# A streamed product-key layer: 84 tokens by index instead of 80, four row blocks instead of eight, a third of v in one fp32 pass

## The reference

```
q = (x @ w_q).reshape(T, 8, 2, 128)
s = einsum('thpd,pnd->thpn', q, sub_keys)         # 128 keys on either side
... top 16 of each side, top 16 of their sums     # 8 heads x 16 = 128 experts for each token
a  = gelu(einsum('td,tkd->tk', x, u[experts])) * gates
y  = einsum('tk,tkd->td', a, v[experts])          # u, v: 16384 rows of 1024, for each layer
```

## Time and profile before

| | us |
|---|---|
| median of 3 runs | 1576.46 (1574.13 to 1580.11) |
| the profiled execution: time | 1579.14 |
| the profiled execution: span | 1577.3 |
| TensorE busy | 1549.5 (98%) |
| VectorE busy | 1355.4 (86%) |
| ScalarE busy | 629.8 (40%) |
| GpSimd busy | 606.9 (38%) |

### The profile page before, as it was taken

How to read it: one execution, slowest core, us unless ns; L and a number is a source line. 1 busy time by engine, 2 the same in 40 slices (tenths; PEclk the granted TensorE clock), 3 DMA queues, 4 the chain that set the end, 5 groups by cost and what they waited for, 6 DMA issues and landing times. The chain is left out here.

```text
span 1577.3 us, 28052 instructions
## 1 busy us (share of the span) xinstructions
PE 1549.5 (98%) x10766; PEld 1494.5 (95%) x10766; DVE 1355.4 (86%) x2569; ACT 629.8 (40%) x1157; POOL 606.9 (38%) x438
## 2 busy tenths in 40 slices
PE   8999999999999999999999999999999999999998
PEld 8988999999999999999888899999999999999996
DVE  6987997989998998888956779898999888888895
ACT  4563222333334444544635341233333344444452
POOL 5651005644442555454003200265444435555520
PEclk9999999999999999999999999999999999999999
DMA  7644579999999999999833247799999999999990
GB/s 244 237 137 135 189 222 359 376 395 372 372 383 378 372 406 408 403 404 404 315 113 109 79 133 254 266 388 375 379 384 376 374 361 409 406 404 407 403 366 27
DMA packets 136965, 493.95 MB, mean 313 GB/s; under 512 B 16064, under 2 KB 16576, under 8 KB 136576
## 3 DMA queue, kind: packets, MB, share of 16 engines
q1 hardware_dynamic: 85248, 307.42, 52.3%
q0 software_dynamic: 47552, 170.06, 27.9%
q10 hardware_dynamic: 4032, 14.68, 2.6%
HBM read 488.79 MB, written 1.05 MB: 311 GB/s over the span
## 5 line engine op out<-in xcount | busy, mean ns | idle before, releaser
L690 POOL DMA_INDIRECT big<-v,picks x160 | 259.0, 1619 | 262.8 <-DVE big L1952 206.5
L690 POOL DMA_INDIRECT big<-u_rows,picks x160 | 220.4, 1377 | 245.9 <-DVE big L1868 217.3
L624 DVE TENSOR_TENSOR low<-raw,high 128x1024 fp32r<-128x1024 f32 x176 | 220.3, 1255 | 38.3 <-ACT high L1262 33.3
L728 PE MATMUL work<-columns,raw 128*128 128x176 f32 x1600 | 249.0, 313 | 3.2 <-DVE big L1846 3.2
L728 PEld LDWEIGHTS work<-columns,raw 128*128 128x128 f32 x1600 | 240.2, 190 | 3.7 <-issue 3.7
L1262 ACT ACTIVATE high<-raw 128x1024 fp32r<-128x1024 f32 x192 | 200.5, 1047 | 40.4 <-PE work L793 9.9
L1952 DVE SCALAR_TENSOR_TENSOR big<-big,side_hid 128x1024 f32<-128x1024 f32 x156 | 199.5, 1279 | 2.3
L1868 DVE SCALAR_TENSOR_TENSOR big<-big 128x1024 f32<-128x1024 f32 x160 | 190.4, 1218 | 9.3 <-DMA big<-u_rows,picks 9.3
L728 PE MATMUL work<-columns,extra_raw 128*128 128x176 f32 x1088 | 174.6, 317 | 5.0 <-DVE big L1846 4.3
L1530 ACT ACTIVATE xT<-big 128x176 fp32r<-128x176 f32 x198 | 67.5, 349 | 268.5 <-PE work L873 204.6
L728 PEld LDWEIGHTS work<-columns,extra_raw 128*128 128x128 f32 x1088 | 166.3, 193 | 5.5 <-issue 4.6
(11 more groups left out here) (262 smaller groups left out, 2881.8 us busy)
## 6 DMA issues: line engine op xcount, KB each, us to landing
raw<-u SPq DMA_DIRECT2D x150, 512.0 KB
raw<-v SPq DMA_DIRECT2D x146, 512.0 KB
extra_raw<-v SPq DMA_DIRECT2D x110, 512.0 KB
extra_raw<-u SPq DMA_DIRECT2D x106, 512.0 KB
raw<-wq SPq DMA_DIRECT2D x32, 512.0 KB
raw<-conv_in SPq DMA_DIRECT2D x14, 512.0 KB
aux<-ln_par ACTq DMA_DIRECT2D x9, 512.0 KB, 8.8
raw<-conv_out SPq DMA_DIRECT2D x8, 512.0 KB
```

What stands on the lines that cost most here:

```text
L624: ops.tensor_tensor(low_at(c), raw_at(c), high_at(c).bitcast(F32), ALU.subtract).then_inc(low_made[RAW_SLOT[c]], 1)
L690: nc.gpsimd.indirect_dma_start(out=side_rows[n % SIDE_BUFS], out_offset=None, in_=rows, in_offset=bass.IndirectOffsetOnAxis(ap=pick_ids[:, ...
L728: mm = nc.tensor.matmul(out_, raw_at(c)[:, k * P:(k + 1) * P], x_full[:, k, :], start=(k == 0), stop=(k == KD - 1))
```

## The change

It moves four tokens (`DT` 172) from the streamed to the gathered side. The second set has 20 tokens in six groups, and 128 experts in six groups make 22 gathers, the last not full; 120 of its 128 partitions are used, and the indices of the other eight are zero. Gathers for each layer go from 80 + 80 to 86 + 86. The batches of gates stay 22, the last with half its tokens left out. `TAIL` goes from 8 to 4, so four blocks of v for each layer are taken as column blocks instead of in rows. Every third block of v is whole (39 instead of 29), and 29 instead of 27 pairs of u. What each part computes stays the same.

```
-SETS = ((64, 2), (16, 8))
+SETS = ((64, 2), (20, 6))
-SET_ROWS = [PH * TOPK // _groups for _, _groups in SETS]
+SET_ROWS = [-(-PH * TOPK // _groups) for _, _groups in SETS]
+SET_USED = [_n * _groups for _n, _groups in SETS]
-BATCHES = DT // BATCH
+BATCHES = -(-DT // BATCH)
+GT = BATCH * BATCHES
-FULL_PAIRS = {5, 14, 23, 33, 42, *PAIR_OF}
+FULL_PAIRS = {5, 12, 18, 25, 33, 40, 47, *PAIR_OF}
-TAIL = 8
+TAIL = 4
-FULL_V = [_n for _n in range(FIRST_COLUMNS, COLUMNS - LAST_COLUMNS) if _n % 4 == 3]
+FULL_V = [_n for _n in range(FIRST_COLUMNS, COLUMNS - LAST_COLUMNS) if _n % 3 == 1]
-TURN_AFTER = (4, 2)
+TURN_AFTER = (4, 3)
+def pick_pieces(i, g):
+    lo, hi = SET_ROWS[i] * g, min(SET_ROWS[i] * (g + 1), PH * TOPK)
+    return [(a, b) for a, b in ((lo, min(hi, P // 2)), (max(lo, P // 2), hi)) if a < b]
...
+            nc.gpsimd.memset(picks[:], 0.0).then_inc(side_filled, 1)
+            nc.gpsimd.memset(side_hid[:], 0.0).then_inc(side_filled, 1)
...
             def add_sides(m):
-                for pick, total in zip(selector, side_sum):
-                    nc.tensor.matmul(y[:, 2 + m, :], pick, total[:, m * 512:(m + 1) * 512],
+                for pick, total, used in zip(selector, side_sum, SET_USED):
+                    nc.tensor.matmul(y[:, 2 + m, :], pick[0:used], total[0:used, m * 512:(m + 1) * 512],
...
             def combine_tail(first, norm, wait_block, wait_half=None):
+                count, slot = (TAIL, COLUMNS) if norm % 2 == 1 else (KD, 0)
```

More of the change, by code:

```diff
@@ L97 @@
 assert len(BATCH_OF) == BATCHES and len(SIDE_SUMS_AT) == SIDE_ROWS
+def pick_pieces(i, g):
+    lo, hi = SET_ROWS[i] * g, min(SET_ROWS[i] * (g + 1), PH * TOPK)
+    return [(a, b) for a, b in ((lo, min(hi, P // 2)), (max(lo, P // 2), hi)) if a < b]
+PICK_LOADS = [sum(len(pick_pieces(_i, _g)) for _g in range(SETS[_i][1])) for _i in range(len(SETS))]
 def set_of(d):
@@ L287, in gated_tokens @@
 def gated_tokens(pair):
-    return BATCH * sum(p <= pair for p in PAIR_OF)
+    return min(DT, BATCH * sum(p <= pair for p in PAIR_OF))
 def program(nc, x_rows, x_cols, positions, conv_par, diag, mla_par, ln_par, keys, w_uq, w_uk, w_uv,
@@ L667, in _ @@
                 pool.wait_ge(own_picked, layer + 1)
+                pool.wait_ge(side_filled, 2)
                 def fetch_picks(i, g):
[L670 to L674, removed]
+                    n, first_row = SETS[i][0], SET_ENDS[i] - SET_ROWS[i]
+                    for a, b in pick_pieces(i, g):
+                        half, to = divmod(a, P // 2)[0], first_row + a - SET_ROWS[i] * g
+                        at = a - half * (P // 2)
+                        nc.gpsimd.dma_start(
+                            picks[n * g:n * (g + 1), :, to:to + b - a],
+                            own_picks[SET_AT[i]:SET_AT[i] + n, :, half, at:at + b - a]).then_inc(picks_in[i], 16)
                 def fetch_tokens(i, g):
@@ L683, in _ @@
                     fetch_tokens(0, g)
-                pool.wait_ge(picks_in[0], 16 * SETS[0][1] * (layer + 1))
+                pool.wait_ge(picks_in[0], 16 * PICK_LOADS[0] * (layer + 1))
                 def gather(n):
@@ L924, in combine_tail @@
             def combine_tail(first, norm, wait_block, wait_half=None):
+                count, slot = (TAIL, COLUMNS) if norm % 2 == 1 else (KD, 0)
                 def part(n, halves, sides=range(2)):
-                    return combine_block(n, first + n, n == 0, n == TAIL - 1, halves, sides)
-                for n in range(TAIL):
+                    return combine_block((slot + n) % KD, first + n, n == 0, n == count - 1, halves, sides)
+                for n in range(count):
                     wait_block(first + n)
@@ L931, in combine_tail @@
                         pe.wait_ge(columns_sum, KD * (norm // 2) + 2)
-                    if norm % 2 == 1 and n == TAIL - 1:
+                    if norm % 2 == 1 and n == count - 1:
                         pe.wait_ge(columns_sum, KD * (norm // 2 + 1))
@@ L937, in combine_tail @@
                 mm.then_inc(y_half, 1)
-                combine_second_half(part, norm, range(TAIL), TURN_AFTER[min(norm, 1)], wait_half)
+                combine_second_half(part, norm, range(count), TURN_AFTER[min(norm, 1)], wait_half)
             def turn_part(n, h, part):
@@ L1936, in combine @@
                     step(V.memset(selector[i], 0.0))
[L1937 to L1938 removed]
+                    used = n * groups
+                    last = V.tensor_reduce(selector[i][0:used, SET_AT[i]:SET_AT[i] + n],
+                                           ident[0:used, 0:used].rearrange("p (g t) -> p t g", t=n), AX.X, ALU.add)
                 last.then_inc(selector_ok, 1)
                 def side_weighted(d):
[L1942 to L1943 removed]
+                    used = SET_USED[set_of(d)]
+                    n, total = before + SIDE_ROWS + d, side_sum[set_of(d)][0:used]
+                    weight = side_hid[0:used, d:d + 1]
                     if d == 0:
```

32 lines of the change are left out of this document (16 added, 16 removed).

## The result

The changed kernel takes 1590.47 us (median of 5, 1588.51 to 1593.67) beside 1578.15 of the kernel before (5 runs on the same chip): ratio 1.0081 [1.0065, 1.0097]. It is 0.8% slower. The forecast was 1563.3 us, faster, and its range ended at 1578: the kernel went the other way and past the end of the range. The profiled span went from 1577.3 to 1588.2 us.

What follows compares the result with a forecast made beforehand. The prediction took TensorE, 98% busy, as the bound, with the DMA engines close behind. Terms -20.0 (TensorE), +1.0 (end of layer 0) and +5.8 (DMA) sum to -13.2 us: 1563.3 us, own range 1556 to 1568, with rivals 1556 to 1578.

Steps and rivals of the forecast that it cites:

- TensorE, four tokens fewer: Matmuls in u and v: 0.053 us less for a whole block, 0.027 for a split one, narrow matmuls unchanged.
- no effect: Rival for TensorE's matmuls: 172 columns take the time of 176, so TensorE gains nothing; 1578 us, chance 0.05.
- v rows: Row stage of v: four row blocks become column blocks, each saving 0.61 us, -2.4 us a layer.
- The end of layer 0: Layer 0 to the next: fewer row matmuls hide the turn of x, so its first matmuls wait about +1.0 us.
- The DMA engines in v: Blocks 4 to 113 of v: 6.9 us missing a layer at 411 GB/s, reserve covers 4.0, +5.8 us in all.
- no reserve: Rival in v: all 6.9 us missing a layer show, +13.8 instead of +5.8; 1571.3 us, chance 0.20.
- 423 GB/s: Rival in v: the engines carry the wanted 423 GB/s, so nothing is missing; 1557.5 us, chance 0.17.
- 402 is the limit: Rival in v: 402 GB/s is all the engines carry, 12.5 us over TensorE's time; 1582.5 us, chance 0.12.
- VectorE in u: Stage u: VectorE's load grows +1.9 us on 174 of 190 us, hidden by TensorE's pace, at no cost.
- The DMA engines in u: Stage u: six more transfers on 185, 381 becomes about 400 GB/s, under 411, with no loss.
- VectorE becomes the bound in u: Rival in u: +1.9 us a layer at 91% busy doubles the 7.5 us of waits; 1571 us, chance 0.06.
- all hidden: Rival in v: the engines carry 423 GB/s or the reserve is 6.9 us; 1557.5 us, chance 0.17.

Runs made afterwards that it cites:

- before_quarter_narrow: The kernel before, with every fourth gather (20 of 80 in either pass) bringing 256 B a partition; 1577.57 us, ratio 0.9992.
- quarter_narrow: The changed kernel with every fourth gather (21 of 86 in either pass) bringing 256 B a partition; 1570.99 us, ratio 0.995.
- kinds_alone: The kernel before with only the new choice of whole blocks in u and v, old sets and eight row blocks; 1585.71 us, ratio 1.0048.
- six_narrow: The changed kernel with six of the 86 gathers of either pass bringing 256 B a partition instead of 4 KB; 1577.47 us, ratio 0.9993.
- half dots: The changed kernel, all gathers whole, with dots over 512 of the 1024 channels; 1578.45 us, ratio 0.9996.
- quarter_narrow_short_dots: The changed kernel with every fourth gather at 256 B a partition and dots over 512 of the 1024 channels; 1555.5 us, ratio 0.9847.
- after_half_gathers: The changed kernel with every gather after the first five of a layer bringing 64 of 128 partitions' rows; 1701.17 us, ratio 1.0782.
- after_gather_120: The changed kernel with the second set's 22 gathers bringing only the 120 used rows; 1694.95 us, ratio 1.073.
- after_late_set: The changed kernel with the second set's small loads issued from gather 30 on instead of 8; 1585.54 us, ratio 1.0043.

## Why the prediction was wrong

**TensorE, four tokens fewer: right where TensorE was free to show it.** A whole block in v, with its first split one:
```profile
1301.04 1.36 PE L898 MATMUL y<-big,extra_raw 128*128 128x172 f32 x8
...
1303.28 0.91 PE L885 MATMUL y<-xT,high 128*128 128x344 f32 x4
...
1305.53 0.83 PE L885 MATMUL y<-xT,high 128*128 128x344 f32 x4
```
The whole block takes 2.24 us and the next 2.25, where the earlier trace rows had 2.29 and 2.26: 0.05 and about 0.01 less in this place (0.053 and 0.027 forecast). Over the whole stage, v columns without the stall (before_quarter_narrow and quarter_narrow) went from 270.3 to 276.6 and 276.3, +6.3 and +6.0; the forecast was -2.5 and four blocks of 2.18 more, +6.2. The rival "no effect" is out.

**v rows: right.** 10.9 us less, 11.2 forecast. Kinds: right in v, as kinds_alone shows; in u VectorE paid for them, and the clock hid it.

**The end of layer 0: about right.** L854 starts at 805.72 after the rows' last matmul of about 805.1, 0.6 us late; 1.0 forecast.

**The DMA engines in v: the deficit was right, the reserve wrong.** The forecast had 6.9 us missing in each layer at 411 GB/s and 4.0 of them covered by slots. The stall is 283.2 - 276.6 = 6.6 and 283.1 - 276.3 = 6.8: the cover gave 0.3 and 0.1. At the 409 GB/s that were reached the same sum has 8.2 us missing, and the cover gave 1.6 and 1.4. Either is below the 1.8 that the forecast took as the least. The rival "no reserve" is close to what happened in v. The step that failed is "a transfer takes between 5.2 and 9.3 us, at the middle two blocks are spare". The 5.2 came from loads of `diag` that ScalarE's queue issues in another stage. In kinds_alone, whose v is not stalled, the page has 8.5 and 7.5 us from issue to landing:
```profile
raw<-v SPq DMA_DIRECT2D x132, 512.0 KB, 8.5
extra_raw<-v SPq DMA_DIRECT2D x124, 512.0 KB, 7.5
```
Once more is wanted than is carried, they take longer. The kernel after:
```profile
raw<-v SPq DMA_DIRECT2D x132, 512.0 KB, 11.9
extra_raw<-v SPq DMA_DIRECT2D x124, 512.0 KB, 10.4
```
In a slot cycle of 15.5 us with 3.8 of use, a landing after 11.2 us (their mean) leaves 0.5 us, by the forecast's own sum. The ceiling was right to within 0.5%: 409 GB/s over 40 us, 411 assumed. The rivals "423 GB/s" and "402 is the limit" are out: 409 is below the one and above the other, and six_narrow runs unstalled at 402. The pauses came by way of ScalarE, as forecast, but earlier: TensorE has some from 600 us of the span on (39.5 of 40 us busy), a third into the stage, not in its last third, and the largest at its end. The Trainium skill (DMA: Bandwidth & Descriptors, Where 436 GB/s comes from) has 358 GB/s for HBM to SBUF and 435 for the fabric. The lower one is a stack's rate divided by two cores, and here one core runs. Neither is the bound that these runs show: 402 to 409 GB/s.

**VectorE in u: the step that decided.** The forecast said that this costs nothing ("what hides it is TensorE's own pace"), and priced the rival at +7.5 us in all with a chance of 0.06. Late u was to shrink by 3.5 us a layer (the rest of the 5.1 lies before) and grew by 3.6 and 2.8. That is 13.4 us in all, half of the miss; 9.7 of it show as longer waits for the gating. I read VectorE's 91% as a mean with room. But the gating that frees TensorE's banks stands in one queue behind whole dots and a batch's tables. A split pair with two dots (2.6 us), two low parts (2.4), the cross addition and the gating (0.9) asks 5.9 us of VectorE in TensorE's 4.4, and a batch's tables 3.1 more, even when the mean doesn't. With 86 dots instead of 80, 33 instead of 27 of the pairs from the seventh on have two (counted in the kernels' tables). The runs show the cause in that half dots gave back 8.1 and 4.8 us a layer; but this is not VectorE's part alone, as said above. That the wait grows in u was written down as "wrong in kind", and so it was.

**The DMA engines in u: wrong too.** The sum used one rate, 411 GB/s. While the second set's small loads run the rate is 354 to 368 GB/s, and the kernel after, with its transfers up by 3%, fell behind there: VectorE waits 6.3 us for gathers in that stretch, before not at all. The late set gave back 4.0 and 3.0 us a layer, 1.7 of either by the clock.

**The early part of u** was to gain 1.6 us a layer and gained 0.3 (77.3 from the first u matmul to the first spread, 77.6 before): PE waits 3.8 us for L1813 in both layers together, 0.9 before. What TensorE saved it waited for VectorE, which prepares the gates there.

**The sum.** Against the forecast's own stages, v columns took 3.7 and 4.7 us more (12.8 and 13.8 longer, 9.1 forecast), late u 7.1 and 6.3, early u 1.3 twice, rows 0.3 twice: 25.0 us; the end of layer 0 took 0.4 less, and what stands before u 0.6 less. That is 24.0 of the 24.1 us by which the span missed its 1564.1. The rest of the 27.2 us is the median: before was 1.7 us higher in this comparison, and the median moved by 1.4 more than the span. The two rivals "no reserve" and "VectorE becomes the bound in u" came together, and even their sum, 1571.3 + 7.5 = 1578.8 us, falls short, since the latter was priced too low. With both bounds out of the way, quarter_narrow_short_dots is at 1555.5 us, the "all hidden" rival's 1557.5: what TensorE would save was forecast well, and neither of the other two could follow.

**Open.** How much of the wait in u of the kernel after is late gathers and how much VectorE's own queue. Late u fell by 8.1 and 4.8 us for half dots, 5.5 and 1.4 for a quarter narrow, 4.0 and 3.0 for the late set, 12.6 and 9.3 for half dots with a quarter narrow. Of these, the stretch at the lower clock is 1.7 in layer 0 of the second and in both layers of the last two. Without it the first two, 8.1 + 3.8 and 4.8 + 1.4, nearly add up to the last, 10.9 and 7.6; but half dots also bring the gathers forward, so this gives no clean shares. And why transfers of few partitions slow the others, which no run took apart.

## What to carry to other kernels

Where a second resource runs at 98% of its best stretch, count its deficit in full: slots that look spare at today's landing time are eaten when the queue is saturated (7.5 and 8.5 us from issue to landing became 10.4 and 11.9). A mean busy share of 91% in an engine that must answer within a few us is not room; lay out its queue for the worst pair, and see who stands ahead of the instruction that the bound engine waits for. Ask also whether what that queue holds in front waits for a load itself. Moving work paid here: fewer row blocks 0.3%, and a whole pair at the tight place 2.8 us of late u in each layer.

## What the runs showed of the hardware

- Indirect gathers over 64 or 120 of 128 partitions lowered the total rate at a DMA share of 1.03: 268 GB/s (after_half_gathers, 300 to 500 us), 290 (560 to 760 us) and 275 (after_gather_120), where whole ones run at 389 to 404 (1.00 to 1.02). The Trainium skill (DMA: Bandwidth & Descriptors, Why a DMA increments its semaphore by 16 and not by 1) has a transfer use the largest number of engines up to 16 that divides its slowest dimension. For 120 partitions that would be 15 and for 64 it would be 16, as for 128: it does not account for a rate lower by a third. Whether it bears on indirect gathers at all, no run here shows.
- While GpSimd's small loads over 16 or 20 partitions ran, the total rate was 353 to 368 GB/s, and 408 with them moved away.
- The wait of TensorE of 2.05 us in the kernel after was followed by a stretch at the lower clock, 1.2 GHz. Its window:
```profile
301.00:305.00 4.00, 3.77 (x17) 3.80 (x17) 2.45 (x4) 0.00 (x0) 1.35 (x1) 0.57 1.04 334
```
The eight matmuls behind that wait took 2.50 us, where eight such take 1.5 elsewhere. Behind the wait of 1.30 us in quarter_narrow, shown above, sixteen took 2.57: no such stretch. Nor is a wait of 2 us always followed by one. In after_late_set the clock stayed at 2.4 GHz behind this:
```profile
1136.43 1.51 PE L765 MATMUL work<-xT,high 128*128 128x344 f32 x8 [2.29 <-DVE big L1867]
```
